# Attention outputs turned with the identity, the high and low halves added on VectorE from PSUM

## The reference, cut to what matters

```python
s = jnp.einsum('bqhd,bkhd->bhqk', qi, k).astype(jnp.float32) * scale
s = s + cqi[..., :, None] - ck[:, :, None, :]
p = jax.nn.softmax(jnp.where(mask, s, -jnp.inf), axis=-1)
return jnp.einsum('bhqk,bkhd->bqhd', p.astype(v.dtype), v)
```

## Time and profile before

| | |
|---|---|
| median of 3 runs | 2849.11 us (2848.85 to 2851.32) |
| the profiled execution | 2857.14 us, its span 2855.4 us |
| busy in the span: PE, DVE, ACT, POOL | 94%, 60%, 41%, 56% |
| busy from 600 to 1100 us, of 500: PE, DVE, ACT, POOL | 447, 398, 366, 445 us |
| granted TensorE clock there | 0.99 of full |
| ends of chunks | 48, from 575 to 1175 us |

### The profile page before, as it was taken

How to read it: one execution, slowest core, us unless ns; L and a number is a source line. 1 busy time by engine, 2 the same in 40 slices (tenths; PEclk the granted TensorE clock), 3 DMA queues, 4 the chain that set the end, 5 groups by cost and what they waited for, 6 DMA issues and landing times. The chain is left out here.

```text
span 2855.4 us, 42028 instructions
## 1 busy us (share of the span) xinstructions
PE 2694.7 (94%) x15009; PEld 2420.7 (85%) x15009; DVE 1710.6 (60%) x2248; ACT 1172.0 (41%) x1961; POOL 1611.1 (56%) x907
## 2 busy tenths in 40 slices
PE   8999999889898898899889999999999989999998
PEld 7998989777777776677789999999999987888887
DVE  5375686487877787676475557665756553224332
ACT  4212312477677777533343334333433332113222
POOL 3476688498899888465466666676655620000111
PEclk9999999899999999999999999999999999999999
DMA  6587889656565666776533333323256347445553
GB/s 211 172 271 243 271 266 316 154 146 166 160 167 159 167 169 174 214 231 211 165 122 106 119 103 126 118 88 119 87 112 153 95 119 205 126 134 162 167 161 110
DMA packets 451021, 468.87 MB, mean 164 GB/s; under 512 B 121959, under 2 KB 347042, under 8 KB 449782
## 3 DMA queue, kind: packets, MB, share of 16 engines
q1 hardware_dynamic: 431662, 443.82, 53.2%
q10 hardware_dynamic: 18864, 21.32, 2.1%
q0 software_dynamic: 288, 1.05, 0.1%
HBM read 384.96 MB, written 81.14 MB: 163 GB/s over the span
## 5 line engine op out<-in xcount | busy, mean ns | idle before, releaser
L2514 PE MATMUL ps_gate_up<-h_hi,w_hi 128*128 128x344 f32 (+1 forms) x1848 | 593.9, 321 | 27.1 <-DVE h_lo L2429 8.9
L2516 PE MATMUL ps_gate_up<-h_hi,w_lo 128*128 128x344 f32 (+1 forms) x1848 | 593.9, 321 | 0.0
L2515 PE MATMUL ps_gate_up<-h_lo,w_hi 128*128 128x344 f32 (+1 forms) x1848 | 593.5, 321 | 0.0
L2514 PEld LDWEIGHTS ps_gate_up<-h_hi,w_hi 128*128 128x128 f32 x1848 | 350.0, 189 | 31.2 <-issue 13.2
L2515 PEld LDWEIGHTS ps_gate_up<-h_lo,w_hi 128*128 128x128 f32 x1848 | 350.2, 190 | 0.0
L2516 PEld LDWEIGHTS ps_gate_up<-h_hi,w_lo 128*128 128x128 f32 x1848 | 350.1, 189 | 0.0
L878 PE MATMUL ps_proj<-w_hi,h_hi 128*128 128x428 f32 (+1 forms) x800 | 288.6, 361 | 9.9 <-ACT proj_out L602 9.8
L879 PE MATMUL ps_proj<-w_lo,h_hi 128*128 128x428 f32 (+1 forms) x800 | 285.0, 356 | 0.0
L880 PE MATMUL ps_proj<-w_hi,h_lo 128*128 128x428 f32 (+1 forms) x800 | 284.3, 355 | 0.0
L2836 PE MATMUL ps_down<-wd_hi,act_hi 128*128 128x512 f32 x704 | 275.6, 392 | 5.9 <-DVE wd_lo L2745 5.9
L1583 DVE TENSOR_TENSOR p_lo<-ps_turned,p_hi 128x512 fp32r<-128x512 f32 (+1 forms) x352 | 213.9, 616 | 102.2 <-ACT p_hi L1475 101.0
(11 more groups left out here) (337 smaller groups left out, 6340.1 us busy)
## 6 DMA issues: line engine op xcount, KB each, us to landing
stock<-in_cache_k SPq DMA_DIRECT2D x192, 256.0 KB, 3.4
common<-in_cache_v SPq DMA_DIRECT2D x172, 256.0 KB, 3.0
common<-in_w_gate SPq DMA_DIRECT2D x33, 1024.0 KB, 6.2
common<-in_w_up SPq DMA_DIRECT2D x33, 1024.0 KB, 6.1
stock<-act_turned SPq DMA_DIRECT2D x16, 1408.0 KB, 8.1
act_raw<-act_turned SPq DMA_DIRECT2D x16, 1408.0 KB, 7.8
page_v<-in_cache_v SPq DMA_DIRECT2D x84, 256.0 KB, 3.0
common<-in_w_in SPq DMA_DIRECT2D x44, 428.0 KB, 4.6
```

The lines of the kernel that those rows point to most:

```text
L2514: pe.matmul(acc, a_hi, h_hi[:, m, d, 0:n], start=d == 0, stop=False)
L2515: pe.matmul(acc, a_hi, h_lo[:, m, d, 0:n], start=False, stop=False)
L2516: mm = pe.matmul(acc, a_lo, h_hi[:, m, d, 0:n], start=False, stop=d == H - 1)
```

## The change

The fold becomes four transposes of full width with the identity. The bank then holds, for each query row, the 64 sums with the high values beside the 64 with the low ones, 512 columns in place of 256. DVE adds the two halves with a reduction over an innermost axis of two, whose elements lie 64 apart in PSUM, and writes `o_out`; a second DVE instruction then multiplies `o_out` with the reciprocals in place. The bank is freed after the addition (`o_summed`). The wait for the reciprocal moves behind the addition, and the product also waits for the addition. The constant `fold` goes away, with two small copies at the start.

```diff
-    dve.tensor_copy(c.fold[0:HD, :], c.ident[0:HD, 0:HD])
-    dve.tensor_copy(c.fold[HD:P, :], c.ident[HD:P, HD:P])
...
-                    take(("fold", k), s.o_out, k + 1)
+                    take(("fold", k), s.o_summed, k + 1)
...
-                            mm = pe.matmul(out[:, r * HD:(r + 1) * HD], a.o_t[:, k % 2, r * P:(r + 1) * P], c.fold[:], start=True, stop=True)
+                            mm = pe.transpose(out[:, r * P:(r + 1) * P], a.o_t[:, k % 2, r * P:(r + 1) * P], c.ident[:])
...
                         dve.reciprocal(a.inv[:, part], a.sums[:, parity, part]).then_inc(s.inverted, 1)
-                        dve.wait_ge(s.inverted, k + 1)
                         dve.wait_ge(s.o_ready, k + 1)
                         if u.head:
                             dve.wait_ge(stored[u.ch], 16 * u.head)
-                        dve.tensor_tensor(a.o_out[:, u.ch, :, :], ps_t[:, bank_of["fold", k], 0:QCH * HD].rearrange("p (r d) -> p r d", d=HD),
+                        turned = ps_t[:, bank_of["fold", k], :].rearrange("p (r h d) -> p r d h", r=QCH, h=2)
+                        dve.tensor_reduce(a.o_out[:, u.ch, :, :], turned, AX.X, ALU.add).then_inc(s.o_summed, 1)
+                        dve.wait_ge(s.inverted, k + 1)
+                        dve.wait_ge(s.o_summed, k + 1)
+                        dve.tensor_tensor(a.o_out[:, u.ch, :, :], a.o_out[:, u.ch, :, :],
                                           a.inv[:, part].unsqueeze(2).to_broadcast([P, QCH, HD]), ALU.mult).then_inc(s.o_out, 1)
```

More of the change, by code:

```diff
@@ L1131, in attend @@
         ps_o = psum("ps_out", [P, BLK])
-        names = ("low_zeroed in_turned k_hi in_hi in_lo turned t_hi t_lo pv scored min made probs v_hi v_lo o_copied o_ready inverted o_out row_made row_out "
+        names = ("low_zeroed in_turned k_hi in_hi in_lo turned t_hi t_lo pv scored min made probs v_hi v_lo o_copied o_ready inverted o_summed o_out row_made row_out "
                  "q0 q1 k0 k1 v0 v1 decay page0 page1 page2 weighed halved added st0 st1 st2 st3 row_st0 row_st1 "
@@ L2875, in decoder_step @@
                   page_before=y_first[:, 0:P], seq_of_page=early_sb("seq_of_page", [P, 2, DB]),
-                  fold=early_sb("fold", [P, HD]), ones=early_sb("ones", [P, 1]),
+                  ones=early_sb("ones", [P, 1]),
                   pages=early_sb("pages", [1, DB * PAGES], I32), page_index=early_sb("page_index", [P, 2], U32),
```

## The result

The changed kernel takes 2903.95 us, the median of 5 runs (2897.74 to 2907.21); the kernel before, on the same chip, 2851.32 (5 runs, 2848.85 to 2857.60). The ratio is 1.0171, 95% interval 1.0155 to 1.0188: 1.7% slower, some 49 us. The profiled execution took 2897.7 us with a span of 2896.0, against 2855.4 in the profile before: 40.6 us more.

What follows compares the result with a forecast made beforehand. TensorE was busiest, 94% of the span, with DVE setting its pace at folds. Fox heads 49 us plus mem heads 4.5 made 53.5, added to the median 2849.1: 2903, with 2864 to 2922 at 8 in 10 or a little more.

Steps and rivals of the forecast that it cites:

- Where to look: Attention-stage folds: DVE's added time reaches PE through waits for `q_lo`, `first_low` and `probs`; PE idle some 70 us more.
- the dear reduction: DVE's reduction of 512 elements from PSUM at the strided SBUF price, 1.16 us.
- TensorE's 0.45 us a fold: PE's fold: four transposes in 0.44 us instead of 0.81 to 0.86, saving 0.40 to 0.45; 0.45 taken.
- The reduction: DVE at each fold: summing pairs 64 apart in PSUM takes 1.16 us, with 0.69 kept as the alternative.
- rival 1: DVE's reduction takes 0.69 us, all else alike: fox heads 34.6 us, mem heads +3, total 2887; chance 0.30.
- The wait for POOL: DVE's product, with two SBUF operands, waits until POOL's current operation ends: 1.2 us more per fold on average.
- What reaches TensorE: DVE's extra time less slack, by kind of fold, never below PE's own -0.45: 49 us in fox heads.
- Mem heads: Folds of mem heads, where DVE itself waits for the fold: +4.5 us in all, between -2 and +10.
- the cheap reduction: DVE's reduction of 512 elements at the price of a sequential read, 0.69 us.
- D: DVE's extra time per fold: 1.1 + 1.2 = 2.3 us, or 1.85 with the cheap reduction.
- rival 2: DVE's product doesn't wait for POOL: 10.7 us more, 2860; with the cheap reduction -4, 2845; chance 0.10.
- Rival 4: DVE's load stays hidden and PE's shorter fold carries: 21.6 us faster, 2827.5; chance 0.04.

Runs made afterwards that it cites:

- the lighter POOL: POOL's page work cut down, that work left out, in both kernels: 0.9983 of before in the changed kernel, 0.9972 in the kernel before.
- the product first: Changed kernel with VectorE's two operations swapped: product in place in PSUM, then the reduction into SBUF; 1.0097 of the kernel before.
- the product in four: Changed kernel with the one product cut into four multiplications of 64 elements by a scalar per partition; 1.0668 of before, 3040 us.
- TensorE's part: Kernel before with the four transposes, VectorE multiplying only the high half from PSUM, low halves not added; 0.9957 of before.

## Why the prediction came out right, and where its steps were not

- **Where to look, right.** VectorE's delay reaches TensorE through `q_lo`, `first_low` and `probs`. PE's waits for these three in the stage grew from 10.9, 4.6 and 12.7 us to 22.8, 18.3 and 20.9; its idle time in the stage grew from 637.5 - 557.5 = 80 us to 680.5 - 552.4 = 128, by 48 (forecast 70, with the dear reduction).
- **TensorE's 0.45 us a fold**, right, with some luck: 0.81 became 0.36. The rows that the forecast shows give 0.81 - 0.44 = 0.37; the new transposes were faster than the 0.44 of those it read.
- **The reduction, wrong.** It takes 0.66 us, not 1.16: the forecast took the dear price from the earlier trace rows and kept 0.69 as rival 1. This term was too large by 0.5 us a fold, by the prediction's own sum 16 us. That pairs would go at the dear price in PSUM is not borne out: 0.69 us there as in SBUF, at every distance.
- **The wait for POOL, right.** Mean in the fox heads 1.05 us for a forecast of 1.2, from 0 to 3.3 us. The long products end 0.28 to 0.29 us behind POOL's operation.
- **What reaches TensorE, right.** Last chunks in full, first ones less 0.67 (measured 0.65), second ones less 0.83 (0.70), third ones less 1.29 (1.23). The wait fell unevenly: mean extras of 2.0 us at second and third chunks and 1.3 to 1.55 at the others. The extras of the 32 fox folds less these slacks add up to 34.0 us, where rival 1, which has the reduction's price, forecast 34.6. The steps add up to 37.9. Two things that the forecast put at nothing make the difference.
- **The split of the values** was shorter than before at third chunks, which takes 5.1 us from the sum. In the fox heads it takes 1.23 to 3.32 us in the kernel before and 1.21 to 1.33 in the changed one; why it met POOL less often there is not shown.
- **The granted clock** adds some 10 us: the folds at which it differs stand 9.8 us above what extras, slacks and the split of the values make, so 34.0 - 5.1 + 9.8 - 0.8 = 37.9, the 0.8 at one fold without a cause that I know. At last, first and second chunks of fox heads the steps of the changed kernel follow from the extras to 0.05 us, but for eight folds, and in seven of these eight the granted clock is not that of the kernel before. The very first fold is one of them, with 1.6 us. The largest is at 842 us: an extra of 3.02 and a step of 5.45. TensorE waits for `q_lo`, and from there to the next fold it has the same 26 operations as before the change. After, then before (columns as in the earlier trace rows):

```profile
848.33 1.11 PE L1404 MATMUL ps_turned<-ident,probs 128*128 128x128 f32 x4 [3.16 <-DVE q_lo L1560]
```

```profile
848.33:855.14 6.81, 6.81 (x26) 6.04 (x27) 4.93 (x9) 2.12 (x4) 6.69 (x3) 0.55 1.25 223
```

```profile
836.65:841.03 4.38, 4.17 (x26) 3.57 (x27) 4.38 (x8) 2.74 (x6) 4.22 (x3) 1.00 1.16 225
```

They take 6.81 us at a granted clock of 0.55, close to the lower of its two levels (1.2 and 2.4 GHz), where they took 4.38 at 1.00. The difference is 2.43 us, the whole surplus of this fold. Over whole executions the granted clock follows TensorE's waits: medians of 0.984 before and with the lighter POOL, 0.981 with the product first, 0.978 in the changed kernel, 0.955 with the product in four. A wait alone does not decide it: behind one of 3.37 us at 944.8 the clock stays at 1.00. So the price of the lower clock is shown, and that it comes with the waits; when a wait brings it is open.
- **Mem heads.** From the first fold there to the last the shift grew by 7 us (forecast 4.5, or 3 with the cheap reduction; for the two folds beside a busy POOL it took 1.6 us where its own D - 0.45 is 1.85). POOL's page work ended 36 us later (1187 against 1151), so that more products of mem heads met it; this I had not counted. The last four steps were 0.40 to 0.46 us shorter, as forecast.
- So 2903 was met by a term too large, the reduction, against one that was missing, the clock, and others too small. That the number is nearer than its steps is luck. Rival 1, with its 2887, had the reduction's price, and the profiled execution would suit it (40.6 us more, forecast 38); the five runs' ratio does not.
- **Rivals 2 and 4** fall with the product's scatter. Their arithmetic can be held against the kernels that make their cases: without the wait, at 0.69 us extra, 3 us where rival 2 said -4; at 1.10 us, 28 where it said 11. Rival 4's 21.6 us of gain is 12 even with no extra at all.
- **Open:** the profiled pair differs by 40.6 us and the medians by 49 to 53. The two profiled executions lie on opposite sides of their medians, and no profile shows what an execution nearer the median does otherwise.

No kernel here that does the whole work beats the one before. TensorE's part did, with part of the output left out. By the table TensorE's 0.5 us is there for an extra near zero. With reduction and product both on VectorE the extra is 0.66 us at best: nothing is gained at first and second chunks, and last ones lose 0.66 each.

## What to carry to other kernels

- Before an operation is added to VectorE beside a busy GpSimd, count its operands in SBUF. Here the second one, four numbers a partition, cost 38 of 49 us, and moving it to PSUM took them away.
- Count what a wait of TensorE does to its granted clock: here some 10 of 38 us in the fox heads came on top of the waits.
- Work moved from the busiest engine to one close behind it is paid at that one's slack. Measure the slack by kind of place (0, 0.65, 0.70 and 1.2 us here) and count only what exceeds it; the gain on the busiest engine counts only where the other leaves room.
- Take the price of an access pattern from a row with the same memory and the same run of elements, or give both prices their chance.

## What was not expected of the hardware

- Four scalings of 64 elements, SBUF to SBUF, took 0.74 us, or up to 8.24 beside POOL: more, smaller operations of this kind multiply the wait.
- A long reduction over elements 8 apart costs 1.07 us for 512 from SBUF and 0.69 from PSUM, while pairs cost 0.69 from either at distances 1, 8 and 64.
- Four transposes of 128x128 fp32 take 0.36 us on TensorE, four matmuls with a 128x64 operand 0.81.
- Four ScalarE scalings of 64 elements in SBUF take 0.34 us each.
